# A hybrid decoder trunk on eight cores: six changes to the order of work, the banks and the loads

## The chip, the cores and the metric

The kernel runs on the 8 cores of one Trainium2 chip. Each core computes one quarter of one of two sequences by itself; no core sends anything to another. The metric is device time in microseconds (us) of the slowest core. A core has TensorE (PE, matrix products, writes PSUM), VectorE (DVE), ScalarE (ACT), GpSimd (POOL, which here only issues weight loads), and SyncE (SP, which here only issues the other transfers). PSUM has 8 banks; each matrix product group of this kernel fills one.

## The reference

```
h = concat(meta tokens (16), x)                       # (2, 16 + 8192, 1024)
for i in range(4):
    a = rms_norm(h, norm_mix[i])
    mixer i mod 3:  0  sliding-window attention, 16 heads, 4 KV heads, window 128, 16 meta keys, sinks, T5 bias
                    1  [B, C, u] = a @ w_in;  z = C * u
                       conv[t] = w0 * z[t-2] + w1 * z[t-1] + w2 * z[t];  out = (B * conv) @ w_out
                    2  trailing means over 2/4/8/16 positions minus the token, per-group linear, scale
    h = h + mixer(a)
    b = rms_norm(h, norm_ffn[i])
    h = h + (silu(b @ w_gate) * (b @ w_up)) @ w_down     # 2816 hidden
out = rms_norm(h, norm_final)[:, 16:]
```

## The kernel before

**Tiling.** A core holds its residual stream (16 meta tokens, a halo of 144 tokens, 2048 tokens) in SBUF in float32, features on partitions in 8 chunks of 128. The columns are worked on in three passes, each of two tiles: 416 and 256 columns in the first pass, 384 and 384 in the other two (`PASS`). Four layers times three passes are 12 steps `i`; layers 0 and 3 are attention, 1 convolution, 2 pooling. Every product is a group of 7 or 8 matmuls (128 x 128 weights, one tile of columns) accumulated in one bank (`group`, line 535). Weights come as units of 448 or 512 KB through a ring of six slots (`load_unit`, line 385), issued on GpSimd's queue; a load waits until TensorE is done with its slot.

**Order.** Nothing is scheduled at run time: `Prog.op` appends every instruction to its engine's list in program order with the semaphore waits it needs, and each engine works through its list in order. So an instruction whose input is late holds up everything behind it on its engine. `_run(main, side, share)` (line 191) interleaves two lists of steps: the side steps are spread evenly over `share` of the cost of the main steps.

**Norms** (`norm_steps`, line 396). A norm of a tile is a list of small steps: 11 statistics steps, the root, 8 scalings. Statistics: ScalarE squares chunk k; in the form `square4`, VectorE adds four squares up and TensorE sums over partitions with a matrix of 1/1024 at k = 6 and k = 10; in the form `square`, TensorE sums each chunk three steps (`LAG`) after its square. The root is two ScalarE operations on the sum, and each scaling is one VectorE operation. These steps are side steps beside matrix products.

**Feed-forward.** It comes in three parts of 8, 7 and 7 chunks of the hidden size. A gate step (`ffn_gu`, line 547) is a gate group and an up group of one tile in two banks, and what follows. Usually that is one Silu and one product. In the stages where attention runs beside (`beside`, line 1201, flag `gate_ln`), silu is made of Exp, Ln and Exp on ScalarE, so that one table of functions serves, and of two VectorE products; the four banks 0 to 3 are for these groups, 4 and 5 for scores, 6 for attention outputs, 7 for norms. A down step (`ffn_dn`, line 581) is one group and its addition to the residual stream, in the order chunk 0 tile 0, chunk 0 tile 1, chunk 1 tile 0, and so on.

**Attention core** (`attn_core`, line 837). An item is 64 queries and two KV heads. Two side steps belong to it: `front(i)` and `back(i-2)`, then `weigh(i)` and `mid(i-1)`. `front` writes scores into two score banks, and ScalarE takes Exp in place; `weigh` multiplies them on VectorE with the bias table into `Pt`, which frees the two banks; `mid` writes outputs and denominators into one output bank, and ScalarE inverts the denominators by Ln and Exp; `back` multiplies on VectorE, which frees the output bank. In the first attention stage (line 1273) there are three score banks and one output bank.

**Convolution** (`conv_in`, line 1025). A step is three groups (B, C, u) of one tile in three banks, which rotate over banks 0 to 5. ScalarE copies u out of its bank to `sgt`; VectorE copies two carried columns into `zt`, multiplies C by u into `zt`, copies the last two columns of `zt` away for the next tile, scales, adds two taps, and multiplies by B. In the first pass the scalings and statistics of a feed-forward norm are side steps.

**Loads of x.** SyncE issues tile 0, small tables, the left halo, tile 1, the bias tables, and then tiles 2 and 3 of x; tiles 4 and 5 wait until the queries of the first tile are written.

The functions that the diff touches:

Of the kernel before, what the change touches and what calls it, by code (L numbers as in the profile page):

```python
# [9 lines left out]
ALU = mybir.AluOpType  # L10

D = 1024
KC = 8
# [19 lines left out]
_I = _Rec()  # L33
# [173 lines left out]
def build():  # L207
    nc = bass.Bass("TRN2", target_bir_lowering=False)
    P = Prog()
# [60 lines left out]
    NSQ = 4  # L270
    LAG = 3
    sq = sb("sq", [128, NSQ, TMAX], BF16)
    sqf = sb("sqf", [128, 3, TMAX])
# [87 lines left out]
    for b in small:  # L361
        b.lw = ("s4", P.cnt["s4"])
    for i in (2, 3):
        x_load(i, ("x", i))

    def load_rest():
        for i in (4, 5):
            x_load(i, ("x", i), reads=tk("gbf", 7, 0, 32))

# [26 lines left out]
    def norm_steps(hsrc, hkeys, n, g, dst, dkeys, quads=True):  # L396
# [15 lines left out]
        def square(k):  # L412
            if k == 0:
                setup()
            if k < KC:
                si = ctr["sq"] % NSQ
                ctr["sq"] += 1
                st["sq"][k] = si
                P.op("act", _I.activation(out=sq[:, si, 0:n], in_=hsrc(k), func=AF.Square),
                     reads=hkeys(k), writes=[B("sq", si)])  # L420
            j = k - LAG
            if j >= 0:
                total(st["sq"][j], j == 0, j == KC - 1)

        def square4(k):
            if k == 0:
                setup()
                st["f"] = {}
            if k < KC:
                f = ctr["sqf"] % 3  # L430
                ctr["sqf"] += 1
                st["f"][k] = f
                P.op("act", _I.activation(out=sqf[:, f, 0:n], in_=hsrc(k), func=AF.Square),
                     reads=hkeys(k), writes=[B("sqf", f)])
            j = k - 1
            if 0 <= j < KC and j % 4:
                f = st["f"][j]
                acc = st["f"][j - 1] if j % 4 == 1 else st["acc"]
                if j % 4 == 3:
                    si = ctr["sq"] % NSQ  # L440
                    ctr["sq"] += 1
                    st["sq"][j // 4] = si
                    out, key = sq[:, si, 0:n], B("sq", si)
                else:
                    out, key = sqf[:, f, 0:n], B("sqf", f)
                    st["acc"] = f
                P.op("dve", _I.tensor_tensor(out=out, in0=sqf[:, acc, 0:n], in1=sqf[:, f, 0:n], op=ALU.add),
                     reads=[B("sqf", acc), B("sqf", f)], writes=[key])
            if k in (6, 10):
                total(st["sq"][k // 8], k == 6, k == 10)  # L450

# [13 lines left out]

        steps = [lambda k=k: (square4 if quads else square)(k) for k in range(KC + LAG)] + [root]
        if dst is not None:
# [39 lines left out]
    def norm_ffn(l, p, quads=True):  # L507

        parts = []
        for t in out_tiles(l, p):  # L510
            src, keys = h_tile(p, t)
            steps = norm_steps(src, keys, t[1], gcol("ffn", l), lambda k, t=t: abf[:, k, t[0]:t[0] + t[1]],
                               lambda k, t=t: tk("abf", k, t[0], t[0] + t[1]), quads)[0]
            parts.append((steps[:KC + LAG + 1], steps[KC + LAG + 1:]))
        return parts
# [27 lines left out]

    gate_ln = [False]
    FGRP = ((0, 8), (8, 7), (15, 7))

    def ffn_gu(l, p, g):
# [4 lines left out]
        def step(jj, ti, t):  # L552
# [7 lines left out]
            si = nxt("sgt")  # L560
            if gate_ln[0]:

                S = sgt[:, si, 0:n]
                P.op("act", _I.activation(out=S, in_=ps[bg][:, 0:n], func=AF.Exp, scale=-1.0), reads=[psb[bg]], writes=[B("sgt", si)])
                P.op("act", _I.activation(out=S, in_=S, func=AF.Ln, bias=oneb[:], scale=1.0), reads=[B("sgt", si), B("oneb")], writes=[B("sgt", si)])
                P.op("act", _I.activation(out=S, in_=S, func=AF.Exp, scale=-1.0), reads=[B("sgt", si)], writes=[B("sgt", si)])
                P.op("dve", _I.tensor_tensor(out=S, in0=ps[bg][:, 0:n], in1=S, op=ALU.mult),
                     reads=[psb[bg], B("sgt", si)], writes=[B("sgt", si)])
                P.op("dve", _I.tensor_tensor(out=gbf[:, jj, t[0]:t[0] + n], in0=ps[bu][:, 0:n], in1=S, op=ALU.mult),
                     reads=[psb[bu], B("sgt", si)], writes=tk("gbf", jj, t[0], t[0] + n))  # L570
                return
# [9 lines left out]
    def ffn_dn(l, p, g, tile_major=False):  # L581
# [5 lines left out]
        def step(m, ti, t):  # L587
# [4 lines left out]
            h_add(p, t, m, bank)  # L592
        order = [(m, ti) for m in range(KC) for ti in range(len(tiles))]
        if tile_major:
# [430 lines left out]
    def conv_in(l, p):  # L1025
# [3 lines left out]
        def prelude():  # L1029
            if p == 0:  # L1030
                claim("scr", [B("zt"), B("cacc")])

        def step(c, ti, t):
            n = t[1]
            banks = []
            for part in range(3):
                i = 3 * c + part
                if i // 2 not in slot:
                    slot[i // 2] = load_unit(ci_d[i // 2], 2 * KC * 128)
                bank = nxt("main", main_banks[0])  # L1040
                banks.append(bank)
# [3 lines left out]
            P.op("act", _I.copy(out=sgt[:, si, 0:n], in_=ps[bU][:, 0:n]), reads=[psb[bU]], writes=[B("sgt", si)])  # L1045
            P.op("dve", _I.tensor_copy(out=zt[:, 0:2], in_=zcar[:, c, :]), reads=[B("zcar", c)], writes=[B("zt")])
            P.op("dve", _I.tensor_tensor(out=zt[:, 2:2 + n], in0=ps[bC][:, 0:n], in1=sgt[:, si, 0:n], op=ALU.mult),
                 reads=[psb[bC], B("sgt", si)], writes=[B("zt")])
            P.op("dve", _I.tensor_copy(out=zcar[:, c, :], in_=zt[:, n:n + 2]), reads=[B("zt")], writes=[B("zcar", c)])
            P.op("dve", _I.tensor_scalar_mul(out=cacc[:, 0:n], in0=zt[:, 0:n], scalar1=cw[:, c:c + 1]),  # L1050
                 reads=[B("zt"), B("cw")], writes=[B("cacc")])
            for tap in (1, 2):
                P.op("dve", _I.scalar_tensor_tensor(out=cacc[:, 0:n], in0=zt[:, tap:tap + n],
                                                    scalar=cw[:, tap * KC + c:tap * KC + c + 1], in1=cacc[:, 0:n],
                                                    op0=ALU.mult, op1=ALU.add),
                     reads=[B("zt"), B("cw"), B("cacc")], writes=[B("cacc")])
            P.op("dve", _I.tensor_tensor(out=qt[:, c, t[0]:t[0] + n], in0=ps[bB][:, 0:n], in1=cacc[:, 0:n], op=ALU.mult),
# [78 lines left out]
    def final(p, regions, quads=True):  # L1136

        parts = []
        for t, r in zip(out_tiles(NLAYER - 1, p), regions):
# [9 lines left out]
            def store(i, name=name, quarter=quarter, t=t, y=y, n=n):  # L1149
# [5 lines left out]
                if i == KC // 2 - 1:  # L1155
                    P.alias(quarter, tall(name))
            steps = norm_steps(src, keys, n, gcol("fin", 0), lambda k, y=y, n=n: y[:, k * n:(k + 1) * n],
                               lambda k, quarter=quarter: [quarter[k // 2]], quads)[0]
            ends = [[steps[KC + LAG + 1 + 2 * i], steps[KC + LAG + 2 + 2 * i], lambda i=i, store=store: store(i)] for i in range(KC // 2)]
            parts.append([begin] + steps[:KC + LAG + 1] + sum(ends, []))  # L1160
        return parts
# [104 lines left out]
    for step in prep[0]:  # L1266
        step()
    first, second = attn_in(0, 0, 0)
    queries, keys = attn_in(0, 0, 1)
    _run(first, prep[2] + prep[1], 0.9)  # L1270
    load_rest()
    items = attn_items(0, 0)
    main_banks[0], s_banks[0], o_banks[0], n_banks[0] = MAIN3, (3, 4, 5), (6,), (7, 7)
    core0, core1 = attn_core(0, 0, items[0:15]), attn_core(0, 0, items[15:])
# [157 lines left out]
```

How the kernel before makes its waits and increments, by code:

```python
                def body(e, lst=lst, fw=fw):  # L121
                    for waits, fn, incinfo in lst:
                        for k, v in waits:
                            e.wait_ge(sems[k], v)
                        name, a_, kw_ = fn
                        ins = getattr(e, name)(*a_, **kw_)
                        if incinfo is not None:
                            ins.then_inc(sems[incinfo[0]], incinfo[1])
                    for k in fw:
                        e.wait_ge(sems[k], self.cnt[k])
```

## Time and profile before

| | |
|---|---|
| median of 3 runs | 2833.15 us (2832.92 to 2833.43) |
| the profiled execution, its own time | 2833.94 us |
| its span (slowest core) | 2832.4 us |
| spans of the 8 cores | 2824.4 to 2832.4 us |
| mean granted TensorE clock | 0.990 to 0.994 |
| TensorE busy | 2721.3 us (96%) |
| VectorE busy | 1596.0 us (56%) |
| ScalarE busy | 1117.4 us (39%) |
| moved by DMA | 290.91 MB |

The span is the time from the first to the last instruction of a core. Busy is the time in which an engine had an instruction in execution; matmuls are pipelined, so TensorE's busy time is not time at its peak. The granted clock is the share of 2.4 GHz at which TensorE was let run; 0.5 is the lower level of 1.2 GHz.

### The profile page before, as it was taken

How to read it: one execution, taken by the hardware profiler on the slowest of the kernel's cores; microseconds unless marked ns; L12 is line 12 of the kernel's file. 1: busy time of each engine (PE TensorE's matmuls, PEld its weight loads, DVE VectorE, ACT ScalarE, POOL GpSimd, SP SyncE). 2: the span in 40 equal slices, each digit the busy share in tenths (PEclk: the TensorE clock that was granted, in tenths of full speed). 3: DMA queues.
4: the chain of work that ended last, by engine and by line, in shares of the span. 5: the costliest groups of instructions: out<-in, count | busy, mean ns of one | idle time of the engine just before them, and what ended most of it. 6: DMA issues, size and time to landing. Idle time of an engine off the chain costs nothing.

```text
span 2832.4 us, 53669 instructions; the slowest of 8 cores (2824.4 to 2832.4 us)
## 1 busy us (share of the span) xinstructions
PE 2721.3 (96%) x18214; PEld 1675.6 (59%) x18214; DVE 1596.0 (56%) x3278; ACT 1117.4 (39%) x2274; POOL 280.2 (10%) x532
## 2 busy tenths in 40 slices
PE   5789999998999999999999999999999999999998
PEld 2356565555566566656566666666556776555664
DVE  5666555665445634646657767445555665664444
ACT  5566635551122113112322223234564674661323
POOL 0000000000011011101111111111001111001010
PEclk8899999999999999999999999999999999999999
DMA  9345565555566566655565575756556666546664
GB/s 235 65 75 89 85 98 89 84 88 91 97 102 106 95 112 112 105 103 96 95 109 101 91 124 102 121 98 111 89 89 108 113 106 106 91 87 106 104 123 109
DMA packets 82972, 290.91 MB, mean 103 GB/s; under 512 B 9940, under 2 KB 11924, under 8 KB 81940
## 3 DMA queue, kind: packets, MB, share of 16 engines
q0 software_dynamic: 76032, 265.85, 57.1%
q1 hardware_dynamic: 6676, 21.64, 2.2%
q8 instruction: 154, 2.52, 0.4%
q14 instruction: 110, 0.90, 0.1%
HBM read 544.87 MB, written 8.39 MB: 195 GB/s over the span
## 4 chain that ended last, share of the span: by engine, by line
PE 85%; DVE 7%; ACT 4%; issue 3%; DMA 1%; DVEq 0%; ACTq 0%; SPq 0%; POOL 0%; POOLq 0%
PE ps L126 85%; ACT sb_sgt L126 3%; DVE sb_scr L126 2%; DVE sb_Pt L126 1%; DMA sb_ring<-attn_q 1%; DVE sb_sgt L126 1%; DVE sb_gbf L126 1%; DVE sb_qt L126 0%; DVE sb_abm L126 0%; DMA sb_h<-x 0%; ACT ps L126 0%; DVE sb_sqf L126 0%; DVE sb_abf L126 0%; DVEq L124 0%; ACT sb_rden L126 0%
## 5 line engine op out<-in xcount | busy, mean ns | idle before, releaser
L126 PE MATMUL ps<-sb_abf,sb_ring 128*128 128x384 bf16 (+2 forms) x8608 | 1371.5, 318 | 12.3 <-DMA sb_ring<-attn_q 4.3
L126 PEld LDWEIGHTS ps<-sb_abf,sb_ring 128*128 128x128 bf16 x8608 | 835.8, 98 | 509.2 <-issue 49.4
L126 PE MATMUL ps<-sb_gbf,sb_ring 128*128 128x384 bf16 (+2 forms) x4352 | 699.9, 316 | 3.3 <-DVE sb_gbf L126 3.1
L126 PEld LDWEIGHTS ps<-sb_gbf,sb_ring 128*128 128x128 bf16 x4352 | 417.4, 98 | 254.5 <-issue 25.5
L126 DVE TENSOR_TENSOR sb_gbf<-ps,sb_sgt 128x384 bf16<-128x384 f32 (+2 forms) x528 | 281.8, 534 | 441.6 <-PE ps L126 365.0
L126 ACT ACTIVATE sb_sgt<-ps 128x384 f32<-128x384 f32 (+2 forms) x528 | 248.5, 471 | 657.7 <-PE ps L126 551.2
L126 DVE TENSOR_TENSOR sb_h<-ps,sb_h 128x384 f32<-128x384 f32 (+2 forms) x624 | 330.1, 533 | 245.2 <-PE ps L126 241.5
L126 PE MATMUL ps<-sb_abm,sb_ring 128*128 128x384 bf16 (+2 forms) x1952 | 316.9, 320 | 19.2 <-DVE sb_qt L126 8.8
L126 PEld LDWEIGHTS ps<-sb_abm,sb_ring 128*128 128x128 bf16 x1952 | 188.6, 98 | 142.5 <-issue 38.8
L126 POOL DMA_DIRECT2D sb_ring<-ffn_gu x264 | 140.5, 532 | 1222.3 <-PE ps L126 1211.7
L126 DVE TENSOR_TENSOR sb_sgt<-ps,sb_sgt 128x384 f32<-128x384 f32 (+2 forms) x206 | 106.8, 519 | 241.7 <-ACT sb_sgt L126 228.9
L126 ACT ACTIVATE sb_sqf<-sb_h 128x384 f32<-128x384 f32 (+2 forms) x256 | 120.8, 498 | 282.8 <-DVE sb_sqf L126 200.5
L126 PE MATMUL ps<-sb_qt,sb_ring 128*128 128x384 bf16 (+3 forms) x1136 | 179.8, 316 | 0.0
L126 ACT ACTIVATE ps<-ps 128x512 f32<-128x512 f32 (+2 forms) x270 | 142.1, 565 | 87.7 <-PE ps L126 87.5
L126 DVE TENSOR_TENSOR sb_Pt<-ps,sb_eb 128x512 bf16<-128x512 f32 (+3 forms) x272 | 167.1, 653 | 5.5 <-ACT ps L126 3.3
L126 PEld LDWEIGHTS ps<-sb_qt,sb_ring 128*128 128x128 bf16 x1136 | 110.6, 98 | 62.8
L126 POOL DMA_DIRECT2D sb_ring<-ffn_dn x144 | 76.0, 527 | 693.8 <-PE ps L126 693.5
L126 ACT ACTIVATE sb_sgt<-sb_sgt,sb_oneb 128x384 f32<-128x384 f32 (+2 forms) x206 | 120.2, 583 | 19.6 <-ACT sb_sgt L126 0.7
L126 DVE SCALAR_TENSOR_TENSOR sb_abf<-sb_h,sb_gam,sb_rstd 128x384 bf16<-128x384 f32 (+2 forms) x208 | 113.5, 585 | 22.5 <-ACT sb_rstd L126 22.4
L126 ACT ACT_TABLE_LOAD x51 | 65.4, 1283 | 144.7 <-PE ps L126 133.8
L126 ACT ACTIVATE sb_sgt<-sb_sgt 128x384 f32<-128x384 f32 (+2 forms) x206 | 101.3, 492 | 19.2 <-ACT sb_sgt L126 0.4
L126 ACT ACTIVATE sb_sq<-sb_h 128x384 bf16<-128x384 f32 (+2 forms) x176 | 82.4, 495 | 52.3 <-PE ps L126 33.3
(92 smaller groups left out, 1464.1 us busy)
## 6 DMA issues: line engine op xcount, KB each, us to landing
sb_ring<-ffn_gu POOLq DMA_DIRECT2D x264, 512.0 KB, 5.3
sb_ring<-ffn_dn POOLq DMA_DIRECT2D x96, 448.0 KB, 4.8
sb_ring<-ffn_dn POOLq DMA_DIRECT2D x48, 512.0 KB, 5.4
sb_ring<-conv_in POOLq DMA_DIRECT2D x36, 512.0 KB, 5.4
sb_ring<-attn_q POOLq DMA_DIRECT2D x24, 512.0 KB, 6.3
sb_ring<-attn_o POOLq DMA_DIRECT2D x24, 512.0 KB, 5.3
sb_h<-x SPq DMA_DIRECT2D x4, 1536.0 KB, 29.1
sb_ring<-conv_out POOLq DMA_DIRECT2D x12, 512.0 KB, 5.3
```

Of the source, the lines that this page charges most:

```text
L126: ins = getattr(e, name)(*a_, **kw_)
```

## The change

It has six parts.

1. In the stages with `gate_ln`, the two VectorE products of a gate step are issued in the next gate step, after that step's ScalarE operations. The last step of a part issues its own products at once.
2. The order of the down groups is four chunks of tile 0, the same four of tile 1, then the other four in the same way.
3. A norm's statistics take 15 side steps (`NSTAT`) instead of 12 with the root: 12 for squares and sums, an empty one, the root, an empty one. In the form `square4` TensorE's sums are at k = 7 and k = 11.
4. In the convolution the first group (B) rotates over banks 0, 1, 2, and the other two over banks 3, 4, 5. The two copies of two columns move from VectorE to ScalarE, and the first two columns of `zt` get a name of their own (`zt2`) for the waits.
5. Tiles 2 and 3 of x are issued after the first norm has written its last chunk; tiles 4 and 5 as before.
6. In the first attention stage there are two score banks (3, 4) and two output banks (5, 6).

```diff
-    for i in (2, 3):
-        x_load(i, ("x", i))
-
-    def load_rest():
-        for i in (4, 5):
-            x_load(i, ("x", i), reads=tk("gbf", 7, 0, 32))
+    def load_late(tiles, after):
+        for i in tiles:
+            x_load(i, ("x", i), reads=after)
...
-            if k in (6, 10):
-                total(st["sq"][k // 8], k == 6, k == 10)
+            if k in (7, 11):
+                total(st["sq"][k // 8], k == 7, k == 11)
...
-        steps = [lambda k=k: (square4 if quads else square)(k) for k in range(KC + LAG)] + [root]
+        steps = [lambda k=k: (square4 if quads else square)(k) for k in range(NSTAT - 3)]
+        steps += [lambda: None, root, lambda: None]
...
             if gate_ln[0]:
+                held, late[0] = late[0], None
...
-                P.op("dve", _I.tensor_tensor(out=S, in0=ps[bg][:, 0:n], in1=S, op=ALU.mult),
-                     reads=[psb[bg], B("sgt", si)], writes=[B("sgt", si)])
-                P.op("dve", _I.tensor_tensor(out=gbf[:, jj, t[0]:t[0] + n], in0=ps[bu][:, 0:n], in1=S, op=ALU.mult),
-                     reads=[psb[bu], B("sgt", si)], writes=tk("gbf", jj, t[0], t[0] + n))
+                if held:
+                    held()
+
+                def products():
+                    P.op("dve", _I.tensor_tensor(out=S, in0=ps[bg][:, 0:n], in1=S, op=ALU.mult),
+                         reads=[psb[bg], B("sgt", si)], writes=[B("sgt", si)])
+                    P.op("dve", _I.tensor_tensor(out=gbf[:, jj, t[0]:t[0] + n], in0=ps[bu][:, 0:n], in1=S, op=ALU.mult),
+                         reads=[psb[bu], B("sgt", si)], writes=tk("gbf", jj, t[0], t[0] + n))
+                late[0] = products
+                if jj == nj - 1 and ti == len(out_tiles(l, p)) - 1:
+                    late[0] = None
+                    products()
                 return
...
-        order = [(m, ti) for m in range(KC) for ti in range(len(tiles))]
+        order = [(m, ti) for m4 in (0, 4) for ti in range(len(tiles)) for m in range(m4, m4 + 4)]
...
-                bank = nxt("main", main_banks[0])
+                bank = nxt("convb", (0, 1, 2)) if part == 0 else nxt("convz", (3, 4, 5))
...
-            P.op("dve", _I.tensor_copy(out=zt[:, 0:2], in_=zcar[:, c, :]), reads=[B("zcar", c)], writes=[B("zt")])
+            P.op("act", _I.copy(out=zt[:, 0:2], in_=zcar[:, c, :]), reads=[B("zcar", c)], writes=[B("zt2")])
...
-            P.op("dve", _I.tensor_copy(out=zcar[:, c, :], in_=zt[:, n:n + 2]), reads=[B("zt")], writes=[B("zcar", c)])
+            P.op("act", _I.copy(out=zcar[:, c, :], in_=zt[:, n:n + 2]), reads=[B("zt")], writes=[B("zcar", c)])
...
+    load_late((2, 3), tk("abf", 7, 0, 32))
...
-    load_rest()
+    load_late((4, 5), tk("gbf", 7, 0, 32))
...
-    main_banks[0], s_banks[0], o_banks[0], n_banks[0] = MAIN3, (3, 4, 5), (6,), (7, 7)
+    main_banks[0], s_banks[0], o_banks[0], n_banks[0] = MAIN3, (3, 4), (5, 6), (7, 7)
```

## Rows read from the trace of the kernel before

**Rows 1.** The page: engine totals, and one group of operations (busy, mean ns, idle before).
```profile
PE 2721.3 (96%) x18214; PEld 1675.6 (59%) x18214; DVE 1596.0 (56%) x3278; ACT 1117.4 (39%) x2274; POOL 280.2 (10%) x532
...
L126 ACT ACTIVATE sb_sgt<-sb_sgt,sb_oneb 128x384 f32<-128x384 f32 (+2 forms) x206 | 120.2, 583 | 19.6 <-ACT sb_sgt L126 0.7
```
**Rows 2.** Stretch, length, busy (x) of PE, PEld, DVE, ACT, POOL; PEclk, DMA share, GB/s.
```profile
57.00:183.00 126.00, 98.17 (x675) 53.90 (x675) 78.83 (x165) 73.05 (x163) 7.92 (x15) 0.87 0.43 76
183.00:665.00 482.00, 471.28 (x3267) 281.49 (x3268) 277.91 (x538) 266.83 (x549) 44.17 (x83) 0.99 0.54 89
665.00:730.00 65.00, 51.95 (x358) 34.13 (x357) 48.64 (x120) 10.88 (x25) 6.34 (x12) 1.00 0.53 87
925.00:992.00 67.00, 64.59 (x388) 36.60 (x387) 47.14 (x112) 9.72 (x19) 6.33 (x12) 1.00 0.57 95
1960.00:2560.00 600.00, 587.10 (x4338) 371.80 (x4335) 360.60 (x730) 352.81 (x748) 59.24 (x111) 1.00 0.59 99
```
**Rows 3.** Waits of PE, 57 to 183 us: total us, times, longest.
```profile
PE ps L126 <- DVE sb_gbf L126: 10.7, 12, 1.6
PE ps L126 <- DVE sb_sq L126: 9.1, 7, 2.6
PE ps L126 <- DVE sb_Pt L126: 4.8, 7, 1.0
```
**Rows 4.** Waits of PE, 183 to 665 us.
```profile
PE ps L126 <- DVE sb_Pt L126: 6.7, 15, 2.3
PE ps L126 <- DVE sb_qt L126: 3.8, 4, 2.2
```
**Rows 5.** Waits of PE, 1960 to 2560 us.
```profile
PE ps L126 <- DVE sb_Pt L126: 11.2, 24, 2.1
```
**Rows 6.** Timeline, first convolution: start, length, operation [idle before <-releaser].
```profile
668.03 7.00 PE L126 MATMUL ps<-sb_abm,sb_ring 128*128 128x416 bf16 x48 [1.74 <-DVE sb_qt L126]
...
672.61 0.51 ACT L126 COPY sb_sgt<-ps 128x416 f32<-128x416 f32 x1 [5.86 <-PE ps L126]
...
676.15 0.59 DVE L126 TENSOR_TENSOR sb_qt<-ps,sb_scr 128x416 bf16<-128x416 f32 x1
...
676.89 7.21 PE L126 MATMUL ps<-sb_abm,sb_ring 128*128 128x416 bf16 x48 [1.85 <-DVE sb_qt L126]
```
**Rows 7.** Timeline of PE in an undisturbed stretch.
```profile
2586.49 36.56 PE L126 MATMUL ps<-sb_abf,sb_ring 128*128 128x384 bf16 x224
```
**Rows 8.** Timeline of PE, second convolution: two pairs of steps.
```profile
941.69 8.13 PE L126 MATMUL ps<-sb_abm,sb_ring 128*128 128x384 bf16 x48 [0.19 <-DVE sb_scr L126]
...
950.00 8.13 PE L126 MATMUL ps<-sb_abm,sb_ring 128*128 128x384 bf16 x48 [0.19 <-DVE sb_scr L126]
```
**Rows 9.** Groups by form: VectorE's copies, ScalarE's smallest operation.
```profile
L126 DVE COPY sb_zcar<-sb_scr 128x2 f32<-128x2 f32 x48 | 8.1, 170 | 5.3 <-DVE sb_scr L126 0.5
L126 DVE COPY sb_scr<-sb_zcar 128x2 f32<-128x2 f32 x48 | 7.7, 160 | 0.0
...
L126 ACT ACTIVATE sb_kt<-ps,sb_attb 128x16 bf16<-128x16 f32 x4 | 1.1, 267 | 0.0
```
**Rows 10.** Timeline, feed-forward beside attention, 284 to 287 us.
```profile
284.19 0.55 ACT L126 ACTIVATE sb_sgt<-sb_sgt 128x416 f32<-128x416 f32 x1
...
285.54 0.59 DVE L126 TENSOR_TENSOR sb_gbf<-ps,sb_sgt 128x416 bf16<-128x416 f32 x1
286.05 1.28 DVE L126 TENSOR_TENSOR sb_Pt<-ps,sb_eb 128x512 bf16<-128x512 f32 x2
286.88 0.27 PE L126 MATMUL ps<-sb_qt,sb_kt 64*128 64x256 bf16 x1 [2.27 <-DVE sb_Pt L126]
```
**Rows 11.** Busy time of the stretch behind that stall; the third number from the end is PEclk.
```profile
287.00:292.00 5.00, 4.67 (x25) 2.96 (x25) 1.51 (x4) 2.79 (x6) 0.53 (x1) 0.66 0.01 3
```
**Rows 12.** DMA, 0 to 40 us: SP's queue, packets, MB, share of time.
```profile
q1 hardware_dynamic: 2359, 6.38, 53.0%
```
**Rows 13.** Timeline of PE, first attention stage.
```profile
152.48 0.30 PE L126 MATMUL ps<-sb_Pt,sb_va 128*64 128x256 bf16 x2 [0.91 <-DVE sb_gbf L126]
```

More of the change, by code:

```diff
@@ L271, in build @@
     LAG = 3
+    NSTAT = 15
     sq = sb("sq", [128, NSQ, TMAX], BF16)
@@ L421, in square @@
             j = k - LAG
-            if j >= 0:
+            if 0 <= j < KC:
                 total(st["sq"][j], j == 0, j == KC - 1)
@@ L513, in norm_ffn @@
                                lambda k, t=t: tk("abf", k, t[0], t[0] + t[1]), quads)[0]
-            parts.append((steps[:KC + LAG + 1], steps[KC + LAG + 1:]))
+            parts.append((steps[:NSTAT], steps[NSTAT:]))
         return parts
@@ L540, in group @@
                  reads=[B("ring", s)] + tk(sname, k, t[0], t[0] + t[1]), writes=[psb[bank]], inc=(k == nk - 1))
-    gate_ln = [False]
+    gate_ln, late = [False], [None]
     FGRP = ((0, 8), (8, 7), (15, 7))
@@ L1030, in prelude @@
             if p == 0:
-                claim("scr", [B("zt"), B("cacc")])
+                claim("scr", [B("zt"), B("zt2"), B("cacc")])
         def step(c, ti, t):
@@ L1045, in step @@
             P.op("act", _I.copy(out=sgt[:, si, 0:n], in_=ps[bU][:, 0:n]), reads=[psb[bU]], writes=[B("sgt", si)])
-            P.op("dve", _I.tensor_copy(out=zt[:, 0:2], in_=zcar[:, c, :]), reads=[B("zcar", c)], writes=[B("zt")])
+            P.op("act", _I.copy(out=zt[:, 0:2], in_=zcar[:, c, :]), reads=[B("zcar", c)], writes=[B("zt2")])
             P.op("dve", _I.tensor_tensor(out=zt[:, 2:2 + n], in0=ps[bC][:, 0:n], in1=sgt[:, si, 0:n], op=ALU.mult),
                  reads=[psb[bC], B("sgt", si)], writes=[B("zt")])
-            P.op("dve", _I.tensor_copy(out=zcar[:, c, :], in_=zt[:, n:n + 2]), reads=[B("zt")], writes=[B("zcar", c)])
+            P.op("act", _I.copy(out=zcar[:, c, :], in_=zt[:, n:n + 2]), reads=[B("zt")], writes=[B("zcar", c)])
             P.op("dve", _I.tensor_scalar_mul(out=cacc[:, 0:n], in0=zt[:, 0:n], scalar1=cw[:, c:c + 1]),
-                 reads=[B("zt"), B("cw")], writes=[B("cacc")])
+                 reads=[B("zt"), B("zt2"), B("cw")], writes=[B("cacc")])
             for tap in (1, 2):
@@ L1055, in step @@
                                                     op0=ALU.mult, op1=ALU.add),
-                     reads=[B("zt"), B("cw"), B("cacc")], writes=[B("cacc")])
+                     reads=[B("zt"), B("zt2"), B("cw"), B("cacc")], writes=[B("cacc")])
             P.op("dve", _I.tensor_tensor(out=qt[:, c, t[0]:t[0] + n], in0=ps[bB][:, 0:n], in1=cacc[:, 0:n], op=ALU.mult),
@@ L1158, in final @@
                                lambda k, quarter=quarter: [quarter[k // 2]], quads)[0]
-            ends = [[steps[KC + LAG + 1 + 2 * i], steps[KC + LAG + 2 + 2 * i], lambda i=i, store=store: store(i)] for i in range(KC // 2)]
-            parts.append([begin] + steps[:KC + LAG + 1] + sum(ends, []))
+            ends = [[steps[NSTAT + 2 * i], steps[NSTAT + 1 + 2 * i], lambda i=i, store=store: store(i)] for i in range(KC // 2)]
+            parts.append([begin] + steps[:NSTAT] + sum(ends, []))
         return parts
```

## Prediction

> **What bounds the kernel now.** I read the page first: TensorE is busy for 2721.3 us of the 2832.4 us span [rows 1]. So 111 us of idle time is the most that better ordering can return, plus what stalls cost in clock and in refilling the pipe. The second view is busy time by stretch [rows 2]. TensorE's idle time there is 126 - 98.2 = 27.8 us at 57 to 183 us (first attention, clock 0.87), 10.7 us at 183 to 665 us (two feed-forwards beside attention cores), 13.0 us in the first convolution, 2.4 us in the second (the third looks alike), and 12.9 us at 1960 to 2560 us (three more feed-forwards beside attention). The stretches between are full. VectorE is 58 to 63% busy beside attention, so it has room; what fails there is order. In the first convolution it is 75% busy.
>
> The third view is what TensorE waits for in those stretches. In the first attention stage it is 10.7 us on attention outputs not yet scaled, 9.1 us on sums of squares, 4.8 us on weighed scores [rows 3]; beside the feed-forwards 6.7 + 3.8 us [rows 4] and 11.2 us [rows 5] on weighed scores and scaled outputs. The fourth view, the timeline, says why each wait is there.
>
> All sums are made against the profiled execution: span 2832.4, its own time 2833.94 us (1.5 us around the span). The median of the runs is 2833.15, 0.8 us lower; I subtract the gain from the median.
>
> **Convolution banks and copies.** In the first pass a pair of steps (416 + 256 columns) starts at 668.03 and the next at 676.89: 8.86 us [rows 6]. Undisturbed matmuls of 384 columns come every 36.56/224 = 0.1632 us, 2353 columns per us [rows 7]. The pair has 24 x 672 = 16128 columns, 6.85 us. So 2.0 us per pair is lost, and 1.85 us of it is the idle time before the pair, ended by VectorE's last product (begun 676.15, 0.59 us long) [rows 6]. That product frees the bank of the first of three groups, which six rotating banks give back after two steps. In the second pass a pair takes 950.00 - 941.69 = 8.31 us [rows 8] against 48 x 0.1632 = 7.83: 0.48 lost, 8 pairs, 3.8 us; the third pass the same.
>
> After the change the first group has three banks to itself, three steps of slack, and this wait goes. What is late next: the third group's bank is that of the previous step's second group, freed by the product at the start of the previous chain. From the rows the chain starts with a ScalarE copy (0.51) and that product (0.59): with two handovers about 1.3 us after the previous step's end, while the third group begins 16 matmuls, 1.75 us (256 columns) or 2.8 us, after it. It holds unless VectorE itself is behind. VectorE's work in a first-pass pair: 48.6 us busy in the stretch [rows 2], less 14 steps' copies (4.6, below) and 16 norm scalings of some 0.6 us (9.6), is 34.4 for 7 pairs, 4.9; with ten handovers of an estimated 0.06 us, 5.5. Over 8 pairs that is 44 + 9.6 = 54 us against TensorE's 8 x 6.85 + 1.3 (eight norm sums) = 56. In the half of the stage where the scalings lie, a pair has 5.5 + 2.4 = 7.9 us of VectorE work, 1.05 more than TensorE's: 4 pairs, up to 4.2 us, some absorbed by the third bank; I take 3. Gain in the first pass: 13 - 3 = 10; second and third 2 x 3.8; together 17.6, taken as 18. Bounds: 6 (first pass stays VectorE-bound) and 21.
>
> The two-column copies cost VectorE 0.170 and 0.160 us, 48 times each: 15.8 us leave it [rows 9]. On ScalarE the nearest row is the 16-column one, 0.267 us [rows 9], so at most 96 x 0.267 = 26 us, in stages where ScalarE is 15 to 17% busy (10.9 of 65) [rows 2]. The copy into the tile waits for VectorE's last tap of the step before, and VectorE's scaling then waits for it; between the two VectorE has its last product and the new product, 1.2 us, to cover 0.3. Behind the second copy on ScalarE stand the next step's copy and norm squares, which have a step of slack. Cost nothing; 0.1 us a step, 5 us, if the cover were gone.
> The Trainium skill speaks against this move: "ScalarE: Activation LUTs", Rules for kernel authors, sends simple arithmetic to VectorE, and "Perfetto Trace Analysis", Optimizing Scalar/DVE Operations, gives an access overhead on SBUF of about 93 ns on ScalarE against 60 on VectorE, but allows offloading when VectorE is saturated. The trace agrees on the sign (0.267 against 0.170). By the first rule the move loses 96 x 0.03, about 3 us by the page's figures, if it lay on the path; by the rows it lies beside it.
>
> **Gate products one step later.** Only beside attention. There a gate step gives ScalarE three passes and VectorE two products that wait for the third; VectorE, in order, holds everything else behind them. At 284: ScalarE's output of that chain ends at 284.74, the gate's second product begins 285.54, the weighing of scores 286.05, and TensorE, which needs the scores' bank, starts at 286.88 after 2.27 us idle [rows 10]. A step later the products find their operands ready, and weighing (and output scaling) no longer stand behind a wait. The waits in question are 6.7 + 3.8 [rows 4] + 11.2 [rows 5] = 21.7 us, one or two tenths of a microsecond more in small ones. I expect two thirds gone, 15 us; the rest is the pair of score banks itself. The stall at 286.88 also costs clock: 0.66 over the next 5 us is 1.7 us lost [rows 11]; three stalls exceed 2 us (2.3 and 2.2 are the longest in [rows 4], 2.1 in [rows 5]), two of them gone give 3. Against it: the delayed products hold two of the four main banks longer. TensorE's step i+2 needs them, and before them stand, at worst, a weighing (1.29), an output scaling (0.42) and a norm scaling (0.6); with their own 1.1 that is 3.4 us, against a step of 32 x 0.1632 = 5.2 us at 384 columns but 3.5 at 256. So a few short new waits: -3. Net 15. Bounds: -10 and 28 (all 23.6 us idle and the clock).
>
> **Down groups by four chunks.** Same groups, same count; the last gate tile's product has four groups before it is read instead of one. Waits seen for that are about 1 us in all; it also covers the late last products. Each weight slot of a pair is freed two groups (2.3 us) later, with six slots ahead. 1 us; bounds -1 and 2.
>
> **Norm steps further apart.** Each sum is asked of TensorE one side step later. 9.1 us of such waits in 7 at 57 to 183 us [rows 3], some 1.5 in the first norms that have matmuls beside them; one side step there is worth 0.4 to 0.6 us of matmuls. 8 x 0.45 = 3.6, less 0.5 in the last norm, whose 15 statistics steps now share the same matmuls with more crowding: 3. Bounds 0 and 8.
>
> **x loads later.** Tiles 2 and 3 (3 MB) are now issued after the first norm, near 23.4 us instead of 13.3. SP's queue had moved 6.38 MB by 40 us [rows 12], and what is issued on it before tile 2 adds up to 6.43 MB by its sizes (tile 0 1.70, left halo 0.59, tile 1 1.05, both bias tables 2.62, small tables 0.47). So tile 2's data did not move before 40 us either way: 0. Bounds 0 and 4, the first weights' waits.
>
> **Two output banks at first.** TensorE no longer waits for the scaling of the item before, as 0.91 us at 152.48 [rows 13]: 10.7 us in 12 [rows 3], 8.6 of it before the value products. But the score banks fall from three to two, each item needs two, so scores of item i+1 wait until all of item i is weighed: one tile, 0.65 us, later. 22 items follow another; at 12 of them it shows: 7.8 us. Net +1; bounds -6 and 8.
>
> **Sum.** 18 + 15 + 1 + 3 + 1 + 0 = 38; 2833.15 - 38 = 2795 us.
>
> **Rivals.**
> A. Score banks, not VectorE's order, hold attention back: TensorE still waits for the same two banks, and the delay returns 3, not 15. For it: many of the waits are 0.33 us ones inside a score group, which the order doesn't touch. Against: the long ones stand behind gate products. 38 - 12 = 26: 2807.
> B. The convolution turns from one bank wait to another or VectorE's own work (third group on the product of the step before): 8 instead of 18: 2805. For it: 7.9 us of work in a pair's place of 6.85. Against: copies leave.
> C. More: all stalls beside attention and their clock (28), convolution 19, the first stage 13 with its clock back from 0.87, the rest 1: 61, 2772. For it: 126 us at 0.87 lose 16 us to the clock.
> D. Slower: the four main banks. The delayed products come too late for every gate step. There are 206 of them [rows 1]. Without the products' 18 the other edits give 23; new waits beyond (23 + 18)/206 = 0.20 us a step make the whole slower. At 0.3 us: 62 us, 2833 - 41 + 62 = 2854. Against it: VectorE's 60%.
> E. The parts cancel, the engines' slack being elsewhere: 2832.
>
> **Chances.** Forecast 0.44, A 0.22, B 0.13, C 0.12, D 0.05, E 0.04. A and B together would be 2815. The forecast's own range is 2783 to 2808; 8 in 10 lie in 2776 to 2817, leaving C and D mostly out. About 0.2% (5.7 us) is what can be told from no change: faster 0.91, within 0.04, slower 0.05.
>
> **What would show it.** First convolution: pairs of 7 to 7.3 us and idle under 4 us; the others at 7.85. Beside attention: VectorE's wait for the gate chain nearly gone, TensorE's idle in the two stretches from 23.6 to about 10. At 57 to 183 us: waits on scaled outputs gone, waits on weighed scores grown. First weights as late as before. Wrong would be: a new wait of gate matmuls on gate products of over 0.2 us a step, or convolution pairs still over 8 us.

## The result and the profile after

| | before | after |
|---|---|---|
| median of 4 runs each | 2833.03 us (2832.27 to 2833.43) | 2804.21 us (2803.19 to 2851.39) |
| profiled execution: span of the slowest core | 2832.4 us | 2801.7 us (2799.1 to 2801.7 over the cores) |
| TensorE's idle time in it | 111.1 us | 90.1 us |

The ratio is 0.9897 [0.9878, 0.9917] (in brackets, here and below, its 95% interval): 28.8 us faster, where 38 were forecast. (The 2851.39 is from an execution in which one die had a lower clock; ratios leave such ones out.) The kernel after's engine totals, which answer to [rows 1]; the gate chains' group is unchanged (206 x 584 ns):

```profile
PE 2711.6 (97%) x18214; PEld 1674.1 (60%) x18214; DVE 1584.9 (57%) x3182; ACT 1126.1 (40%) x2370; POOL 280.3 (10%) x532
```

TensorE has the same 18214 matmuls, yet is busy 9.7 us less: some of the gain is matmuls that run at a better clock or less broken up. Windows of the kernel after at the stages of [rows 2]; the last number but two is the granted clock. The last three windows are the first 26.5 us behind the first convolution pass:

```profile
57.00:191.00 134.00, 102.45 (x674) 54.22 (x675) 79.46 (x166) 73.41 (x164) 7.92 (x15) 0.85 0.39 67
191.00:655.00 464.00, 463.40 (x3263) 278.05 (x3261) 276.98 (x535) 264.56 (x549) 44.16 (x83) 1.00 0.56 93
654.00:712.00 58.00, 53.48 (x373) 35.75 (x370) 45.10 (x90) 16.33 (x57) 6.41 (x12) 1.00 0.63 104
915.00:980.00 65.00, 65.00 (x405) 39.41 (x403) 45.27 (x82) 14.44 (x52) 6.86 (x13) 1.00 0.59 102
1940.00:2530.00 590.00, 582.57 (x4353) 370.67 (x4352) 359.54 (x731) 350.93 (x753) 59.50 (x111) 1.00 0.59 101
...
715.00:717.50 2.50, 1.87 (x6) 0.87 (x7) 0.42 (x1) 0.00 (x0) 0.00 (x0) 0.50 0.91 138
717.50:720.00 2.50, 2.50 (x9) 1.18 (x8) 0.00 (x0) 1.56 (x2) 0.00 (x0) 0.50 0.00 0
720.00:742.00 22.00, 22.00 (x133) 13.10 (x132) 4.46 (x8) 4.13 (x9) 2.11 (x4) 0.98 0.41 73
```

Read these first. Idle time beside attention fell from 10.7 to 0.6 us in the first two feed-forwards and from 12.9 to 7.4 in the last three. The second convolution pass has none left. But the first attention stage took 8 us more for the same matmuls (idle 27.8 -> 31.6, busy 98.2 -> 102.5 at a clock of 0.85), and behind the first convolution pass there are 5 us at half clock.

The same landmark instructions in both traces (the slowest core of each; every row is the difference, after less before, that the stretch adds; feed-forwards are numbered by their step `i`, 0 to 11):

| stretch | us |
|---|---|
| start to the first gate chain beside attention (189.06 -> 197.17; median of the 8 cores 187.4 -> 196.8) | +8.1 |
| feed-forward 0 and 1 beside attention | -9.7, -6.8 |
| convolution, pass 1, pass 2, pass 3 | -8.6, -4.1, -4.3 |
| end of convolution pass 1 to the start of pass 2 | +7.1 |
| feed-forward 8, 9, 10 beside attention | +1.0, -9.8, -2.8 |
| all else | -0.8 |
| sum | -30.7 |

So two things gave more or as much as said (beside attention 28, convolution 17), and two took 15 us back.

TensorE's waits in the first attention stage of the kernel after (57 to 191 us; total, times, longest), against [rows 3]:

```profile
PE ps L126 <- DVE sb_Pt L126: 14.5, 22, 2.0
PE ps L126 <- DVE sb_sq L126: 11.6, 7, 3.4
...
PE ps L126 <- DVE sb_gbf L126: 2.1, 2, 1.2
```

Waits for scaled outputs fell by 8.6 us as forecast, waits for weighed scores grew by 9.7 and for sums of squares by 2.5. Its timeline there shows how:

```profile
155.19 1.28 DVE L126 TENSOR_TENSOR sb_Pt<-ps,sb_eb 128x512 bf16<-128x512 f32 x2
...
156.02 0.27 PE L126 MATMUL ps<-sb_gbf,sb_kt 64*128 64x256 bf16 x1 [0.94 <-DVE sb_Pt L126]
...
163.73 0.27 PE L126 MATMUL ps<-sb_gbf,sb_kt 64*128 64x256 bf16 x1 [1.04 <-DVE sb_Pt L126]
...
164.33 0.38 PE L126 MATMUL ps<-sb_gbf,sb_kt 64*128 64x256 bf16 x3 [0.33 <-DVE sb_Pt L126]
164.64 2.92 PE L126 MATMUL ps<-sb_gbf,sb_ring 128*128 128x416 bf16 x8
```

The scores of an item start when the first half of the item before is weighed and wait again (0.33) for the other half, 1.3 us of idle time together. It is so at the items that follow each other directly; at 158.99 and 161.56, where eight matmuls of 416 columns stand between two items, there is no wait. Behind the waits the eight matmuls at 164.64 take 2.92 us; the eight at 157.48 took 1.58.

The timeline behind the first convolution pass, kernel after:

```profile
709.36 1.03 PE L126 MATMUL ps<-sb_abm,sb_ring 128*128 128x256 bf16 x8 [0.48 <-DVE sb_scr L126]
...
713.88 1.07 DVE L126 SCALAR_TENSOR_TENSOR sb_scr<-sb_scr,sb_cw 128x256 f32<-128x256 f32 x2
715.06 0.42 DVE L126 TENSOR_TENSOR sb_qt<-ps,sb_scr 128x256 bf16<-128x256 f32 x1
...
715.63 26.55 PE L126 MATMUL ps<-sb_abf,sb_ring 128*128 128x384 bf16 x146 [5.24 <-DVE sb_qt L126]
```

TensorE waits 5.24 us for the convolution's very last product (it waited 1.86 us there before). The convolution's groups now rotate under their own names (`convb`, `convz`), so the `main` rotation stands where it stood before the pass, and the first gate group takes the bank of the last B group, which is freed last of all. The 146 matmuls behind it would take 146 x 0.1632 = 23.8 us; they took 26.55. Stall and clock together are 3.4 + 2.7 = 6.1 of the 7.1 us.

### The profile page after: what moved, and what is told of

It reads as the page before. It is cut to its first block, busy times and chain, and to the rows that moved or that the text cites. A ratio compares the mean times of both kernels' runs of the same rounds, so it can differ in the third digit from the quotient of the medians.

```text
span 2801.7 us, 53884 instructions; the slowest of 8 cores (2799.1 to 2801.7 us)
## 1 busy us (share of the span) xinstructions
PE 2711.6 (97%) x18214; PEld 1674.1 (60%) x18214; DVE 1584.9 (57%) x3182; ACT 1126.1 (40%) x2370; POOL 280.3 (10%) x532
## 4 chain that ended last, share of the span: by engine, by line
PE 90%; DVE 4%; DMA 2%; ACT 2%; issue 2%; DVEq 0%; ACTq 0%; SPq 0%; POOL 0%; POOLq 0%
PE ps L126 90%; DMA sb_h<-x 1%; ACT sb_sgt L126 1%; DVE sb_Pt L126 1%; DMA sb_ring<-attn_q 1%; DVE sb_scr L126 1%; DVE sb_abf L126 1%; DVE sb_qt L126 0%; DVE sb_abm L126 0%; ACT ps L126 0%; DVE sb_sgt L126 0%; DVE sb_sqf L126 0%; DVE sb_h L126 0%; DVE sb_gbf L126 0%; ACT sb_rden L126 0%
## 5 line engine op out<-in xcount | busy, mean ns | idle before, releaser
L126 DVE TENSOR_TENSOR sb_sgt<-ps,sb_sgt 128x384 f32<-128x384 f32 (+2 forms) x206 | 106.6, 517 | 207.6 <-ACT sb_sgt L126 194.9
L126 DVE TENSOR_TENSOR sb_Pt<-ps,sb_eb 128x512 bf16<-128x512 f32 (+3 forms) x272 | 167.0, 652 | 12.9 <-ACT ps L126 11.3
L126 PE MATMUL ps<-sb_sq,sb_onesb 128*128 128x384 bf16 (+2 forms) x242 | 68.3, 321 | 33.0 <-DVE sb_sq L126 30.3
```

The costliest lines, as they stand in the source:

```text
L126: ins = getattr(e, name)(*a_, **kw_)
```

## The experiments

Each was measured beside the kernel before on the same chip. The first four ran on one chip, only the count, all but the banks and the two that build on it on a second, the others on a third; the kernel before takes 2833.3, 2833.7 and 2834.0 us on them, so differences of a microsecond between chips mean nothing. On the second chip one run of the kernel before at 2858.59 us counts in the ratios, which makes them lower than the times say (2796.82/2833.7 is 0.987) and their intervals wide. "First gate chain" is the landmark at the end of the first attention stage, as the median of the 8 cores (187.4 before). With the same code its time differs from core to core by up to 8 us (184.9 to 192.7 in the run with the convolution part alone), so single cores are not compared there.

**Gate products alone** (part 1 put on the kernel before):

```diff
+                if held:
+                    held()
...
+                late[0] = products
```

> Only the gate products one step later, all else as before. Theory 1, the delay alone clears VectorE's queue beside attention: the five feed-forward stages beside attention give back all that they gave in the changed kernel, about 28 us, most of it in the first, second and fourth; time about 2805 us. Theory 2, as the prediction priced it: 15 us, 2818, and the other 13 us come from the down order or the norm spacing in the same stages. Theory 3, the score banks hold: 3 us, 2830. The first attention stage and the convolutions must stay where they were.

Measured: 2807.86 us, ratio 0.991 [0.9889, 0.9931], 26 us faster. All of it lies beside attention (-9.2, -6.2, +0.5, -9.3, -2.3 in the five feed-forwards). Windows over one of the five, feed-forward 9, from its first to its last gate chain, kernel before:

```profile
2205.00:2346.00 141.00, 133.01 (x1207) 100.77 (x1205) 87.51 (x194) 102.97 (x237) 15.30 (x30) 0.99 0.66 109
```

and gate products alone:

```profile
2188.40:2320.10 131.70, 129.06 (x1207) 99.02 (x1204) 87.48 (x194) 100.79 (x237) 15.30 (x29) 1.00 0.69 114
```

Over all five windows 788.0 us became 761.5. Idle time fell from 20.6 to 5.7, which is 14.9 us. Another 11.6 us is TensorE's busy time, 767.4 -> 755.8 for the same matmuls. Three of the five windows had one stall of over 2 us each and a granted clock of 0.99; now no stall is that long and the clock is 1.00 in all five. That accounts for some 5 us (1% of the 494 us of those three windows; three times the 1.7 us of [rows 11] gives the same). The other 6.6 us no row separates. A part of it should be groups that are no longer broken up: four score matmuls take 0.57 us in one piece (kernel after, 158.99) and 0.27 + 0.38 when a wait parts them. The delayed products held the main banks up by at most 1.4 us in all (4 waits on `sgt`; 0.4 us in 2 before). Waits of TensorE in this kernel, first at 188 to 600 us, then at 1945 to 2550 (columns as above), against [rows 4] and [rows 5]:

```profile
PE ps L126 <- DVE sb_Pt L126: 0.7, 2, 0.3
PE ps L126 <- DVE sb_qt L126: 0.6, 1, 0.6
```

```profile
PE ps L126 <- DVE sb_Pt L126: 5.1, 10, 1.3
PE ps L126 <- DVE sb_sgt L126: 1.4, 4, 0.6
```

So rival A (the score banks themselves) is out for the first two feed-forwards; in the last three it is what is left.

One sign that the prediction named did not show. VectorE still waits for ScalarE's chain at the gate products. The pages of the kernel before and of this one have (busy, mean ns, idle time before and what ended it):

```profile
L126 DVE TENSOR_TENSOR sb_sgt<-ps,sb_sgt 128x384 f32<-128x384 f32 (+2 forms) x206 | 106.8, 519 | 241.7 <-ACT sb_sgt L126 228.9
...
L126 DVE TENSOR_TENSOR sb_sgt<-ps,sb_sgt 128x384 f32<-128x384 f32 (+2 forms) x206 | 106.7, 518 | 212.5 <-ACT sb_sgt L126 205.7
```

The wait is 228.9 us before and 205.7 us here. What changed is what stands behind it: the weighings and scalings of a step are now in VectorE's list ahead of the products, not behind them.

**Convolution alone** (part 4):

```diff
+                bank = nxt("convb", (0, 1, 2)) if part == 0 else nxt("convz", (3, 4, 5))
...
+            P.op("act", _I.copy(out=zt[:, 0:2], in_=zcar[:, c, :]), reads=[B("zcar", c)], writes=[B("zt2")])
```

> Only the convolution's two bank pools and the copies on ScalarE. Theory 1: the pairs of the first pass fall from 8.8 to 7.5 us (9 us), those of the other two from 8.3 to 7.8 (4 us each), and 7 us are given back at once, because the convolution no longer advances the common bank rotation, so the gate group after its first pass gets the bank that the last step's final product frees last; together -10, about 2823 us, with one stall of some 5 us behind the first convolution. Theory 2: that stall of 5 us belongs to the norm spacing or the gate delay; then no stall here and about 2816 us.

Measured: 2823.55 us, ratio 0.9967 [0.9954, 0.998]. Pass 1 -9.2, the stretch behind it +6.9, passes 2 and 3 -4.0 and -4.3: together -10.6 us, which is the run's 10. The stall is there without any other part:

```profile
725.78 24.51 PE L126 MATMUL ps<-sb_abf,sb_ring 128*128 128x384 bf16 x132 [4.88 <-DVE sb_qt L126]
```

**Banks alone** (part 6: one score bank fewer, one output bank more, first stage):

```diff
+    main_banks[0], s_banks[0], o_banks[0], n_banks[0] = MAIN3, (3, 4), (5, 6), (7, 7)
```

> Only two score banks and two output banks in the first attention stage. Theory 1: this is what makes that stage 8 us longer in the changed kernel (waits on weighed scores grew from 4.8 to 14.5 us, waits on scaled outputs fell from 10.7 to 2.1); time about 2839 us, first gate chain at 195 to 197 us instead of 189. Theory 2, the prediction's price: a gain of 1 us, 2832, and the loss is the norm spacing's.

Measured: 2839.78 us, ratio 1.0021 [1.0009, 1.0032], 6 us slower; first gate chain 194.3. Its TensorE waits from 57 to 190 us:

```profile
PE ps L126 <- DVE sb_Pt L126: 15.3, 24, 1.7
PE ps L126 <- DVE sb_sq L126: 10.1, 6, 3.4
...
PE ps L126 <- DVE sb_gbf L126: 2.1, 2, 1.2
```

The trade loses by itself, and the exchange is that of the whole change: 10.5 us more on scores, 8.6 less on outputs.

**Norm steps alone** (part 3):

```diff
+            if k in (7, 11):
+                total(st["sq"][k // 8], k == 7, k == 11)
...
+        steps += [lambda: None, root, lambda: None]
```

> Only the norm steps further apart. Theory 1, the banks cost the first stage its 8 us: here the first stage is 0 to 3 us shorter, waits on sums of squares fall from 9.1 us at 57 to 183 us to 5, time about 2830 us. Theory 2, the spacing costs it: first gate chain at 194 us or later, waits on sums of squares at 11 us or more, time about 2838 us. It also tells whether the spacing gives anything beside the feed-forwards (theory 1: under 2 us).

Measured: 2859.97 us at the lowest, ratio 1.0096 [1.0074, 1.0117], 27 us slower, where the worse of the two theories had 2838. The loss lies beside attention: +7.2 in feed-forward 1, +7.9 in feed-forward 10, +3.1 and +2.0 in 0 and 9. Its TensorE waits, whole run, and then at 430 to 640 us (where the kernel before has 0.7 us in 3 on `Pt`):

```profile
PE ps L126 <- DVE sb_Pt L126: 40.2, 65, 2.3
PE ps L126 <- DVE sb_sq L126: 27.4, 12, 13.8
```

```profile
PE ps L126 <- DVE sb_Pt L126: 5.9, 7, 2.2
```

Whole-run waits on `Pt` are 22.7 us in 46 before. The timeline has one of the new long waits:

```profile
479.20 0.52 ACT L126 ACTIVATE sb_sgt<-sb_sgt 128x384 f32<-128x384 f32 x1
...
479.82 0.56 DVE L126 TENSOR_TENSOR sb_sgt<-ps,sb_sgt 128x384 f32<-128x384 f32 x1 [1.55 <-ACT sb_sgt L126]
...
480.48 0.56 DVE L126 TENSOR_TENSOR sb_gbf<-ps,sb_sgt 128x384 bf16<-128x384 f32 x1
480.96 1.28 DVE L126 TENSOR_TENSOR sb_Pt<-ps,sb_eb 128x512 bf16<-128x512 f32 x2
481.79 0.27 PE L126 MATMUL ps<-sb_qt,sb_kt 64*128 64x256 bf16 x1 [2.23 <-DVE sb_Pt L126]
```

`_run` spreads all side steps evenly, so three more steps in a norm also move every attention step against the gate steps, and a weighing falls behind a gate product that waits for ScalarE. That the 20 us beside attention are of this kind is what the run with gate products and norm steps, below, shows: they go with the late products. Another 5 us lies between the start of feed-forward 3 and that of 8, where no attention runs; its cause stays open.

**Only the count of side steps** (15 statistics steps, TensorE's sums left at k = 6 and 10; the diff is against norm steps alone):

```diff
-            if k in (7, 11):
-                total(st["sq"][k // 8], k == 7, k == 11)
+            if k in (6, 10):
+                total(st["sq"][k // 8], k == 6, k == 10)
```

> The kernel before with the 15 statistics steps (the three empty ones and the root at their new places) but TensorE's sums at k = 6 and k = 10 as before. The norm spacing alone made the kernel 26 us slower. Theory 1, the count of side steps does it, because it shifts where attention steps fall among the gate steps, and a badly placed weighing waits behind gate products: about 2860 us here too, waits on weighed scores at 40 us. Theory 2, the later sums do it, by holding the norm's buffers longer: about 2835 here.

Measured: 2866.04 us, ratio 1.0099 [1.0071, 1.0127]. The count alone costs the 27 us and more. The later sums give back 3 to 5 us of it (lowest time 2863.2 against 2860.0, with each less the kernel before of its chip 31 against 27; waits on `sq` 32.7 us in 17 against 27.4 in 12), about the 3 us that the prediction gave them.

**Gate products and norm steps** (parts 1 and 3):

> The kernel before with the later gate products and the norm spacing, nothing else. Alone they gave -26 and +26 us. Theory 1, the delay takes away what made a badly placed step dear: -26 and +2 to +5 us, that is 2810 to 2813, waits on weighed scores near 11 us. Theory 2, the two add up: 2834.

The edit is the sum of the two diffs above. Measured: 2811.61 us, ratio 0.9921 [0.9901, 0.994]. The two alone add up to 2834; together they are 4 us above gate products alone, a difference that the ratios' intervals do not separate. By the landmarks it lies between feed-forwards 3 and 8 again (+4.2); beside attention the five windows take 759.8 us against 761.5. At 425 to 615 us one wait of 0.2 us on `Pt` is left. With the products late, it does not matter where an attention step falls.

**All but the banks** (part 6 undone):

```diff
-    main_banks[0], s_banks[0], o_banks[0], n_banks[0] = MAIN3, (3, 4), (5, 6), (7, 7)
+    main_banks[0], s_banks[0], o_banks[0], n_banks[0] = MAIN3, (3, 4, 5), (6,), (7, 7)
```

> The changed kernel with three score banks and one output bank in the first attention stage as before. Theory: the two output banks cost that stage 7 us alone (194.3 against 187.4 us, median of the cores, for the first gate chain) and cost it as much in the full change: 2804 - 7 = 2797 us, first gate chain at 189 to 190 us. Rival: the stage's loss is the joint work of the banks and the later sums; then 2801 or more.

Measured: 2796.82 us, ratio 0.9842 [0.9779, 0.9905], 7.4 us below the changed kernel; the first gate chain is at 188.5 us where it was at 196.8.

**And the rotation carried on**, so that the first gate group behind a convolution pass takes the bank after the last B group's, not that bank itself:

```diff
+            rot["main"] = (bB + 1) % 3
```

> The same, and after each convolution step the common rotation is set so that the next gate group takes the first-group bank that was released longest ago. Theory: the stall of 5.2 us behind the first convolution goes and with it the slow clock behind it: 7 us less than the kernel without the bank edit, 2790 us. Rival: the next bank is then the late one and half of the stall stays: 2794.

Measured: 2789.58 us, ratio 0.9816 [0.9752, 0.9879], 7.2 us below the same without the line. From the end of pass 1 to the start of pass 2 it is now 0.9 us shorter than before. Its TensorE timeline there:

```profile
705.33 1.46 PE L126 MATMUL ps<-sb_abf,sb_ring 128*128 128x384 bf16 x8
707.63 16.57 PE L126 MATMUL ps<-sb_abf,sb_ring 128*128 128x384 bf16 x101 [0.84 <-DVE sb_qt L126]
```

One gate group runs at once, the next waits 0.84 us for that product, and the matmuls behind keep their pace (16.57/101 = 0.164).

**Three score and two output banks, two for the other products** (on top of it, first stage):

```diff
+    main_banks[0], s_banks[0], o_banks[0], n_banks[0] = (0, 1), (2, 3, 4), (5, 6), (7, 7)
```

> The same as the kernel before it in this call, but the first attention stage has two main, three score and two output banks. Theory 1, TensorE's order is what binds there and both score and output waits go (10.7 and 4.8 us of waits in the kernel before): 5 us less, 2785. Theory 2, two main banks are too few, since each group then waits for the evacuation of the one two groups before it: 0 to 6 us more, 2790 to 2796.

Measured: 2785.79 us, ratio 0.9803 [0.9684, 0.9923], 3.8 below the one before; and the first gate chain (median of the cores) is at 184.8 us where it was at 189.4. Scores keep their three banks, and outputs get the second; that the two main banks would be too few did not show.

**Without the norm steps**, first the kernel with the rotation and then this last one (parts 1, 2, 4, 5 and the two lines above):

> The kernel with the rotation set after the convolution and the first stage's banks as before (2789.6 us), but without the norm spacing. Theory: under the delayed gate products the spacing is worth little either way, its later sums give 3 to 5 us in the first stage and between the layers, and its empty steps cost 2 to 5: 2788 to 2793. Rival: the spacing still costs 5 us or more; then 2785 or less.

> The fastest kernel so far (two main, three score, two output banks in the first stage, rotation set; 2785.8 us) without the norm spacing. If the spacing is neutral under delayed gate products: 2784 to 2788. If its later sums matter, up to 2791; if its empty steps cost, 2780.

Edit: part 3's diff reversed. Measured: 2787.44 us, ratio 0.9836 [0.9816, 0.9855], and 2783.57 us, ratio 0.9822 [0.98, 0.9844]. Each is 2.1 to 2.2 us below its twin with the spacing, which ran on another chip, and less than a ratio's interval: the spacing is worth nothing in company, or costs 2 us. The last is the fastest of all, 50 us below the kernel before on its chip and some 20 below the changed one. Its TensorE waits at 57 to 182 us:

```profile
PE ps L126 <- DVE sb_sq L126: 10.7, 7, 3.4
PE ps L126 <- DVE sb_Pt L126: 10.0, 13, 1.9
...
PE ps L126 <- DVE sb_gbf L126: 2.1, 2, 1.2
```

Waits on weighed scores are 10.0 us, between the 4.8 of [rows 3] and the 14.5 of the changed kernel, although the scores have three banks as before (the main groups have two instead of three). So of their growth in the change about half comes even with the third score bank kept: where TensorE no longer waits for outputs, it waits for scores instead.

**Down groups and x loads** (parts 2 and 5):

```diff
+        order = [(m, ti) for m4 in (0, 4) for ti in range(len(tiles)) for m in range(m4, m4 + 4)]
...
+    load_late((2, 3), tk("abf", 7, 0, 32))
```

> Only the down groups by four chunks and the later x loads. Theory: 0 for the loads, since the data of tiles 2 and 3 did not move before 40 us anyway, and a gain of 1 to 4 us for the down order, whose waits on gate products (about 1 us outside the first stage) go, beside attention perhaps more: 2830 to 2833. Rival: the later loads move the first weights forward, waits on them in the first 57 us (4.6 us) fall under 2, and the first attention starts 3 us earlier.

Measured: lowest 2832.18 us, where the lowest of the kernel before is 2832.41; there is no ratio. In the trace its marks lie within 0.1 us of before from 431 to 1227 us, and 1.2 to 1.6 us early from 1966 us on; the first gate chain is where it was (median 187.2 against 187.4). So the loads move nothing that can be seen, and the down order is worth some 1.4 us in this one trace, too little for the times to show.

## Why the prediction was right, and by which terms it was off

The kernel is faster and within the forecast's own range, 9.2 us short of the point. By its steps:

- **Convolution, 18: right.** 8.6 + 4.1 + 4.3 = 17.0 in the change, 9.2 + 4.0 + 4.3 = 17.5 alone. A pair of the first pass takes 7.49 us (7 pairs in 52.43; 8.82 before), above the 7 to 7.3 named; in the other passes it is 7.79, where 7.85 was named. What is late is what rival B named, the third group on the product of the step before, but at 2.9 us in 6 waits instead of 10. VectorE's surplus cost no more than the 3 us that it was given. ScalarE's two-column copies take 192 and 195 ns and hide (TensorE has no idle time in the second pass); the bound was 267. For an ACTIVATE with immediate scale and bias the Trainium skill ("ScalarE: Activation LUTs", What ACT_TABLE_LOAD costs) gives 186 ns and 0.833 ns an element; for two columns that makes an estimate of 188 ns. The copies are COPY operations, and the trace has them 4 to 7 ns longer.
- **Gate products later, 15: mis-sized.** 26 us alone; 28.1 beside attention in the change, with whatever the norm steps do there. The order of the queue and the idle time were right (14.9 us net of new waits, where 15 - 3 = 12 were priced; in the change 8.0 us idle in the two stretches where about 10 was expected). But "the products find their operands ready" was wrong: VectorE's wait for the chain was to be nearly gone and is 205.7 us of 228.9 (194.9 in the change). The gain came only from what no longer stands behind that wait. The step that failed is the price of a stall's consequences: "two of them gone give 3". It was 11.6 us: all three stalls of over 2 us went, which is some 5 us of clock, and the other 6.6 us, for which the sum had no term, came as busy time in four of the five feed-forwards. Rival C's 28 for this term was near in number and not in kind: it took all 23.6 us of idle time as gone and the rest as clock. The three-microsecond charge for held main banks was at most 1.4, of which 0.4 was there before.
- **Two output banks, +1: wrong in sign and size.** -6 alone, -7.4 in company. It was right that waits on outputs go (8.6 of the 10.7) and that scores then wait for all of the item before. The charge of 12 items x 0.65 us = 7.8 met 9.7 to 10.5. The waits on scores do not come from the lost score bank alone: with three score banks kept they are still 10.0 us. The step that failed is the netting: it stopped at idle time. Sums of squares came 1 to 2.5 us later, and TensorE's busy time grew 4.3 us for the same matmuls, with the clock at 0.85 instead of 0.87.
- **Missed: the counter.** Own names for the convolution's rotations stop the `main` rotation. The prediction asked which bank is late inside the convolution and not what the first group behind it takes. It costs 7 us: 7.1 in the change, 6.9 alone, 7.2 returned by one line. With it the convolution part gives 10 us of its 18.
- **Norm steps, 3: right only for the sums.** They give 3 to 5 us, but the three extra side steps were costed by their crowding (0.5) and not by where they move the attention steps: 27 us alone, nothing measurable beyond 2 to 4 us once gate products are late. In the change the term is 0 to -4 instead of +3.
- **Down order, 1:** 1.4. **x loads, 0:** 0. TensorE waited 3.4 us for the first weights, 4.6 before (4.3 and 0.3). Rows of the kernel after for SP's queue over the first 40 us, against [rows 12]:

```profile
q1 hardware_dynamic: 2444, 6.53, 53.1%
```

From 38 the point moves by +13 (beside attention), -8 (banks), -7 (counter) and -3 to -7 (norm steps) to 29 to 33; 28.8 was measured. Misses of both signs partly cancelled, so it is in part luck that the sum fell in the range, and its small error flatters the terms. Of the rivals none came out whole. B's 2805 us is nearest to the time measured, and its 8 us to the convolution's 10 with the stall, but by coincidence: the convolution itself gave its 17, and B knew neither the counter nor the banks' loss. What stays open is what the 6.6 us of busy time beside attention consist of, and the 5 us that the extra side steps cost where no attention runs.

## What to carry to other kernels

Where an engine works through its list in order, an instruction that waits for another engine's chain costs not itself but all that stands behind it; putting it a step later in the list, so that other engines' work stands ahead of it, was the largest gain here, although the waiting engine waited nearly as long as before. It also made the kernel insensitive to where attention steps fall. When a rotation of buffers is split or renamed, look at the first user behind the stage, which inherits a counter that stood still. When banks are traded between two uses, count the waits of both uses and then TensorE's busy time too: beside attention 14.9 us of idle time, in waits of up to 2.3 us, came back nearly twofold.

## What the runs showed of the hardware

- Idle time of 5.24 us was followed by 5 us at a granted clock of 0.50 (1.2 GHz) though TensorE was full again: 2.7 us on top. In the variant with 0.84 us of idle time the matmuls behind kept 0.164 us each.
- The clock also fell without any long idle time. In the 30 us before, the longest wait of TensorE is 1.04 us. Behind waits of 1.04 and 0.33 us eight 416-column matmuls took 2.92 us instead of 1.58; the row of the kernel after for those 5 us:

```profile
164.00:169.00 5.00, 4.67 (x23) 2.07 (x24) 1.87 (x5) 1.47 (x4) 0.00 (x0) 0.66 0.00 0
```

- Removing 14.9 us of idle time in 788 us removed 11.6 us of busy time for the same matmuls, some 5 of them by the granted clock (0.99 in three of five windows before, 1.00 now).
- Two-column copies took 192 to 195 ns on ScalarE and 160 to 170 ns on VectorE ([rows 9]).
- The same code reaches the same point of the first stage up to 8 us apart on different cores (184.9 to 192.7 us).
